# Staging the raw blocks of the key table in PSUM, by quarters, and the dots' fixed rows in four banks

## The reference, cut to what matters

```python
best, sel = lax.top_k(cand, PEER_TOPK)            # 8 heads x 16 experts for each token
eidx = jnp.take_along_axis(cidx, sel, axis=-1)
g = jax.nn.softmax(best, axis=-1)
u = jnp.take(u_tab, eidx, axis=0)
a = jax.nn.gelu(jnp.einsum('thkd,td->thk', u, xb).astype(jnp.float32))
vv = jnp.take(v_tab, eidx, axis=0)
return jnp.einsum('thk,thkd->td', (g * a).astype(xb.dtype), vv)
```

## Time and profile before

| | |
|---|---|
| median of 3 runs | 2502.88 us (2501.28 to 2506.49) |
| the profiled execution, its own time | 2504.55 us |
| its span, first to last instruction | 2503.0 us |
| busy: PE, DVE, POOL, ACT | 2275.1, 1816.6, 1172.0, 938.5 us |
| U stage in the profile | about 801 to 1757 us |
| V stage | about 1757 to 2495 us |

### The profile page before, as it was taken

One profiled execution on the slowest core, in us unless ns is written; L12 is line 12 of the kernel. 1 busy time (PEld: TensorE's weight loads), 2 busy tenths in 40 slices (PEclk: granted clock), 3 DMA queues, 4 the chain that ended last, 5 costly groups with the idle time before them and its releaser, 6 DMA issues.

```text
span 2503.0 us, 36629 instructions
## 1 busy us (share of the span) xinstructions
PE 2275.1 (91%) x13843; PEld 2021.0 (81%) x13843; DVE 1816.6 (73%) x2242; ACT 938.5 (37%) x1030; POOL 1172.0 (47%) x618
## 2 busy tenths in 40 slices
PE   7989999899999999777887878778999999999998
PEld 5878778788899999777887878778877777777777
DVE  3555555563468998878776766676789988998988
ACT  4364553533333443323322222233333333333332
POOL 1020100120005877788887887883444454544441
PEclk9999999999999999989998898889999999999999
DMA  5463444477334678899999999999999999999996
GB/s 186 135 194 119 155 141 126 161 290 294 125 114 135 167 209 290 317 327 323 368 336 323 314 325 321 314 319 341 382 411 413 411 413 412 412 412 409 412 413 278
DMA packets 221520, 722.70 MB, mean 289 GB/s; under 512 B 55672, under 2 KB 105624, under 8 KB 154871
## 3 DMA queue, kind: packets, MB, share of 16 engines
q1 hardware_dynamic: 113872, 380.68, 41.1%
q0 software_dynamic: 87408, 318.89, 35.9%
q10 hardware_dynamic: 20151, 22.05, 2.6%
HBM read 679.70 MB, written 41.83 MB: 288 GB/s over the span
## 4 chain that ended last, share of the span: by engine, by line
PE 34%; POOL 23%; DMA 20%; DVE 13%; issue 8%; DVEq 1%; ACT 1%; SPq 1%; ACTq 0%; POOLq 0%
POOL g_dense L478 16%; PE banks L1331 10%; PE banks L1333 10%; PE banks L1332 10%; DMA v_raw<-in_v_tab 9%; POOL u_row L472 7%; DMA a_tile<-a_dense 7%; DVE h L1275 5%; DMA g_dense<-route,route_place 3%; DVE v_lo L1281 2%; DVE ring_lo L1281 1%; DVEq L832 1%; DVE prm L934 1%; DMA raw<-in_w_in 1%; DVE u_lo L1195 0%
## 5 line engine op out<-in xcount | busy, mean ns | idle before, releaser
L478 POOL DMA_INDIRECT g_dense<-route,route_place x256 | 565.8, 2210 | 304.8 <-DVE route_place L1188 175.9
L1333 PE MATMUL banks<-xT_hi,u_lo 128*128 128x256 f32 x2048 | 600.0, 293 | 0.0
L515 POOL DMA_INDIRECT v_row<-in_v_tab,route_place x128 | 340.2, 2657 | 411.9 <-DVE h L1275 364.8
L1235 DVE CUSTOM_DVE_ANT_0 u_row<-u_row,x_rows 128x2048 f32<-128x2048 f32 x128 | 293.2, 2291 | 195.5 <-DMA u_row<-in_u_tab,route_place 193.8
L1333 PEld LDWEIGHTS banks<-xT_hi,u_lo 128*128 128x128 f32 x2048 | 415.0, 203 | 0.0
L854 DVE TENSOR_TENSOR ring_lo<-raw,ring_hi 128x2048 fp32r<-128x2048 f32 x72 | 165.0, 2291 | 216.0 <-ACT ring_hi L542 215.6
L1275 DVE SCALAR_TENSOR_TENSOR h<-v_row,w_values,h 128x2048 f32<-128x2048 f32 x128 | 300.2, 2345 | 0.7
L1331 PE MATMUL banks<-xT_hi,ring_hi 128*128 128x256 f32 (+1 forms) x768 | 236.0, 307 | 29.4 <-DVE u_lo L1195 29.4
L776 ACT ACTIVATE gelu_out<-gelu_out 128x256 f32<-128x256 f32 x128 | 53.4, 417 | 544.5 <-DVE gelu_out L1229 532.3
L1332 PE MATMUL banks<-xT_lo,ring_hi 128*128 128x256 f32 (+1 forms) x768 | 234.6, 305 | 0.0
L1331 PE MATMUL banks<-ring_hi,w_hi 128*128 128x512 f32 x512 | 204.5, 399 | 19.9 <-DVE ring_lo L1281 18.3
(11 more groups left out here) (264 smaller groups left out, 5522.6 us busy)
## 6 DMA issues: line engine op xcount, KB each, us to landing
v_raw<-in_v_tab SPq DMA_DIRECT2D x128, 1024.0 KB, 14.7
u_raw<-in_u_turned SPq DMA_DIRECT2D x64, 1024.0 KB
raw<-in_u_turned SPq DMA_DIRECT2D x64, 1024.0 KB, 5.8
raw<-in_w_in SPq DMA_DIRECT2D x160, 256.0 KB, 3.5
raw<-in_w_out SPq DMA_DIRECT2D x64, 256.0 KB, 4.4
g_dense<-zeros POOLq DMA_DIRECT2D x16, 1024.0 KB, 28.6
raw<-in_w_pq SPq DMA_DIRECT2D x64, 256.0 KB, 3.6
a_dense<-gelu_out ACTq DMA_DIRECT2D x128, 128.0 KB
```

What stands on the lines that cost most here:

```text
L478: pool.indirect_dma_start(out=places, out_offset=bass.IndirectOffsetOnAxis(ap=routeU[:, t, 2, j:j + 1], axis=0), in_=route[:, t, 0, j:j + ...
L515: pool.indirect_dma_start(out=vrow[k % NVB][:, :], out_offset=None, in_=rows, in_offset=bass.IndirectOffsetOnAxis(ap=routeU[:, NT - 1, 1, ...
L1235: V.tensor_tensor_reduce(row[:, :], row[:, :], xrow[:, :], 1.0, 0.0, ALU.mult, ALU.add, adot[:, i:i + 1]).then_inc(dot_done, 1)
L1333: return MM(out, l1, h2, start=False, stop=last)
```

## The change

ScalarE gets a new step, `u_stage(m)`, right behind `u_hi(m)`: it copies the raw block by quarters of 512 columns into PSUM banks 2 and 3 in turn. VectorE's `u_lo(m)` becomes four instructions, each of which takes one quarter from its bank and the high part from SBUF. ScalarE may write a bank again when VectorE is done with the quarter two before. TensorE waits for the quarters one by one. Since banks 2 and 3 are taken, TensorE accumulates in banks 0 and 1 only, and `scaled(m-2)` stands right behind `u_lo(m)`, ahead of routing and dots, in place of `scaled(m-3)` at the end. Blocks 0 and 1 lose their early place among the last sweeps of the stage before. `x_rows`, the operand that all dots share, is copied once (m = 4) into banks 4 to 7, and the dots read it there.

```diff
+        xbank = psum[:, 4:8, :]
...
+            def u_stage(m):
+
+                for i in range(4 * m, 4 * m + 4):
+                    if i >= 2:
+                        act.wait_ge(u_lo_done, i - 1)
+                    A(bank[2 + i % 2], rawu[m % UR][:, i % 4 * W:(i % 4 + 1) * W], ACT.Copy).then_inc(u_bank, 1)
...
-                act.wait_ge(u_scaled, m + (UR + 1))
+                act.wait_ge(u_scaled, m + 3)
...
+            u_stage(0)
             for m in range(1, P):
                 if m >= 2:
                     u_hi(m)
+                u_stage(m)
...
+                if m == UR:
+                    act.wait_ge(x_row, 1)
+                    A(xbank, xrow[:, :].rearrange("p (b x) -> p b x", x=W), ACT.Copy).then_inc(x_bank, 1)
...
                 dve.wait_ge(u_hi_done, m + 1)
-                V.tensor_tensor(uL[m % UR].rearrange("p (b e) -> p b e", e=P), rawu[m % UR].rearrange("p (b e) -> p b e", e=P),
-                                uH[m % UR].bitcast(F32), ALU.subtract).then_inc(u_lo_done, 1)
+                for i in range(4 * m, 4 * m + 4):
+                    dve.wait_ge(u_bank, i + 1)
+                    V.tensor_tensor(uL[m % UR][:, i % 4 * W:(i % 4 + 1) * W].rearrange("p (b e) -> p b e", e=P),
+                                    bank[2 + i % 2].rearrange("p (b e) -> p b e", e=P),
+                                    uH[m % UR][:, i % 4 * 4:i % 4 * 4 + 4, :].bitcast(F32), ALU.subtract).then_inc(u_lo_done, 1)
...
-                V.tensor_tensor(aout[:, m % 2, :], bank[m % UR][:, 0:TU], rootB[:, :], ALU.mult).then_inc(u_scaled, 1)
+                V.tensor_tensor(aout[:, m % 2, :], bank[m % 2][:, 0:TU], rootB[:, :], ALU.mult).then_inc(u_scaled, 1)
...
-                V.tensor_tensor_reduce(row[:, :], row[:, :], xrow[:, :], 1.0, 0.0, ALU.mult, ALU.add, adot[:, i:i + 1]).then_inc(dot_done, 1)
+                V.tensor_tensor_reduce(row[:, :], row[:, :], xbank.rearrange("p b x -> p (b x)"), 1.0, 0.0, ALU.mult, ALU.add, adot[:, i:i + 1]).then_inc(dot_done, 1)
...
             for m in range(P):
+                u_lo(m)
                 if m >= 2:
-                    u_lo(m)
+                    scaled(m - 2)
...
-                if m >= UR - 1:
-                    scaled(m - (UR - 1))
...
                 pe.wait_ge(u_scaled, m + 1)
-                pe.wait_ge(u_lo_done, m + 1)
                 for b in range(KC):
+                    if b % 4 == 0:
+                        pe.wait_ge(u_lo_done, m * 4 + (b // 4 + 1))
```

More of the change, by code:

```diff
@@ L296, in hybrid_layer @@
         row_used = sem("row_used")
+        u_bank = sem("u_raw_in_bank")
+        x_row, x_bank = sem("x_row_ready"), sem("x_bank_ready")
         urow_in = [sem(f"urow_in{i}") for i in range(NUB)]
@@ L849, in _ @@
             dve.sem_inc(lo_done, 2)
-            dve.sem_inc(u_scaled, UR)
+            dve.sem_inc(u_scaled, 2)
             V.memset(epsv, EPS).then_inc(z_done, 1)
@@ L1212, in _ @@
                     V.scalar_tensor_tensor(out=xrow[:, :], in0=hh[:, NT - 1, :], scalar=rrx[:, NT - 1:NT], in1=gbc[:, :],
-                                           op0=ALU.mult, op1=ALU.mult)
+                                           op0=ALU.mult, op1=ALU.mult).then_inc(x_row, 1)
                     drain()
@@ L1216, in _ @@
                     sweep(n)
-                    if s == 15:
-                        u_lo(i)
                 for quarter, part in QUARTER_IN_PQ.get(s, ()):
@@ L1228, in scaled @@
                     dve.wait_ge(root_ev, 1)
-                V.tensor_tensor(aout[:, m % 2, :], bank[m % UR][:, 0:TU], rootB[:, :], ALU.mult).then_inc(u_scaled, 1)
+                V.tensor_tensor(aout[:, m % 2, :], bank[m % 2][:, 0:TU], rootB[:, :], ALU.mult).then_inc(u_scaled, 1)
             def dot(i):
+                if i == 0:
+                    dve.wait_ge(x_bank, 1)
                 dve.wait_ge(urow_in[i % NUB], 16 * (i // NUB + 1))
                 row = urow[i % NUB]
-                V.tensor_tensor_reduce(row[:, :], row[:, :], xrow[:, :], 1.0, 0.0, ALU.mult, ALU.add, adot[:, i:i + 1]).then_inc(dot_done, 1)
+                V.tensor_tensor_reduce(row[:, :], row[:, :], xbank.rearrange("p b x -> p (b x)"), 1.0, 0.0, ALU.mult, ALU.add, adot[:, i:i + 1]).then_inc(dot_done, 1)
             sweep(3 * N_SWEEPS - 1)
@@ L1281, in v_lo @@
                 V.tensor_tensor(vL[m % VS], vraw[m % VS], vH[m % VS].bitcast(F32), ALU.subtract).then_inc(lo_done, 1)
-            scaled(P - 3)
+            scaled(P - 2)
             v_lo(0)
-            scaled(P - 2)
             w_product(0)
@@ L1583, in u_step @@
                 pe.wait_ge(u_scaled, m + 1)
-                pe.wait_ge(u_lo_done, m + 1)
                 for b in range(KC):
+                    if b % 4 == 0:
+                        pe.wait_ge(u_lo_done, m * 4 + (b // 4 + 1))
                     c = slice(b * P, (b + 1) * P)
-                    last = three(bank[q][:, 0:TU], uH[q][:, b, :], uL[q][:, c], xTh[:, b, 0:TU], xTl[:, b, 0:TU], b == 0, b == KC - 1)
+                    last = three(bank[q % 2][:, 0:TU], uH[q][:, b, :], uL[q][:, c], xTh[:, b, 0:TU], xTl[:, b, 0:TU], b == 0, b == KC - 1)
                 last.then_inc(u_used, 1)
@@ L1606, in v_step @@
                     last.then_inc(split_used, 1)
-            pe.wait_ge(u_scaled, P + UR)
+            pe.wait_ge(u_scaled, P + 2)
             pe.wait_ge(wl_done, 1)
```

## The result

The changed kernel takes 2866.97 us (median of 4 runs, 2855.63 to 2867.47) beside 2504.05 us for the kernel before in the same comparison: a ratio of 1.1445, 95% interval 1.1418 to 1.1471. It is 363 us slower. I had forecast 43 us faster; the slowest of my rivals stood at 2538.

The account below looks back on a forecast made before the run. POOL, its indirect DMAs held by VectorE instructions with two SBUF inputs, was taken to set the U stage's pace from 957 us. Terms +16 - 16 - 43 = -43 us gave a forecast of 2460 us, range 2433 to 2500.

Parts of the forecast that it names:

- ScalarE's round: ScalarE's in-order work per U-stage block: about 5.6 us, under PE's 5.75; blocks with one dot lose 0.2 us.
- the signs that I had listed for being wrong: U stage: POOL's durations stay, DMA's share stays 0.94 with POOL idle, or DVE waits for banks over 0.5 us a quarter.
- To block 26: U stage, 801 to 957 us: dearer low parts 13 us, ScalarE's round some 3 us, together +16 us.
- Blocks 26 to 51: U stage, 957 to 1163 us: DVE's own work plus a few waits for rows makes 190 us, -16 us.
- Blocks 52 to 121: U stage, 1163 to 1708 us: DMA is next to bound, 502 us for 545, -43 us, ends -33 to -62.
- My last rival: DMA has more room than its share says; DVE sets step 3 at 434 us, -111, total 2392 us; chance 0.05.
- the price of the quarters: VectorE's low part of a U-stage block in four quarters through two banks: about 2.7 us, taken as +0.5 us a block.
- two accumulators at next to nothing: U stage: VectorE's lead over PE shrinks from three blocks to two; cost put at nothing.
- The passage of the Trainium skill that I set among the rivals: Supports the rival that the change frees nothing: POOL's durations stay, +16 us or so, 2519 us; chance 0.02.
- the hand-over of quarters: Rival, U stage: low parts cost more than taken; at 1.2 us more a block, +35 us, 2538 us; chance 0.07.
- The rival that DMA is the bound already: U stage: POOL's freedom only moves the wait; step 3 gives 0, Blocks 26 to 51 at most -10; 2509 us; chance 0.09.
- step 3: The forecast's term for Blocks 52 to 121, U stage, 1163 to 1708 us: DMA-bound at 502 us, -43 us.

Follow-up runs that it names:

- experiment 3: The changed kernel with gelu(m-3) between u_hi(m) and u_stage(m) on ScalarE, a block earlier, still two gelu_out buffers: 2404.8 us, ratio 0.9608.
- experiment 8: experiment 3 with the low part of blocks 0 to 25 in one instruction from SBUF, unstaged, as in the kernel before: 2392.6 us, ratio 0.9568.
- experiment 4: The kernel before with only the dots' part: x_rows copied once into banks 4 to 7 and read there by the dots: 2432.8 us, ratio 0.9724.
- experiment 6: experiment 3 with the dots reading x_rows from SBUF again, so the staging without the dots' part: 2491.8 us, ratio 0.9944.
- experiment 5: The kernel before with two accumulators in place of four and scaled(m-2) right behind the low part, no staging: 2494.6 us, ratio 0.9964.
- experiment 9: The changed kernel with the dots' rows in SBUF and four staging banks, gelu behind the staging, two gelu_out buffers: 2481.5 us, ratio 0.9912.

## Why the prediction was wrong

**The step that failed** is the last sentence of "ScalarE's round": "`u_hi(m+1)` is queued behind `u_stage(m)`, and `gelu` too; the gelus wait for nobody's sake." Somebody does wait for them. The store that a gelu ends in frees one of two `gelu_out` buffers, and `scaled` needs it. I named what is queued behind the new wait and did not go on from there to who waits for it. All the pieces were there: `scaled` waits for the store of the block two before its own, the stores stand in the timeline, and the change brings `scaled` one block forward while it puts the gelu behind a wait for VectorE. Its price follows from the trace after: gelu 0.4, issue, and landing, 4.9 us from the gelu's start (1508.77) to `scaled` (1513.69), against 0.8 us that VectorE needs from that start to the end of its low part. That is 4.1 us a block, and 4.1 x 117 = 480 of the 495 us. None of the signs that I had listed for being wrong names the store.

**The sum's other terms** can be read in experiment 3, where that wait is gone (span 2405.8, that is -97 us).
1. To block 26: +23 us for +16. Some 17 us lie between the low parts of block 2 and block 26 (153.8 us for 137.2), near what I counted. The other 6 come at the start: block 2's low part begins at 826.3 for 820.0. I named no cost for the start. VectorE stands still for 8.0 us ahead of block 0's low part, since ScalarE comes to its first copies only behind its work for the scores. In experiment 8, with the same order and nothing staged there, block 2 begins at 822.7. So in these profiles about 3 of the 6 us go with the lost place of blocks 0 and 1 and 4 with the staging.
2. Blocks 26 to 51: 187 us for 210, -23 where I had -16.
3. Blocks 52 to 121: 448 us for 545, -97 where I had -43. I took the DMA share as an amount of work, 0.94 x 545 = 512 us. In experiment 3 the share makes 1.04 x 449 = 467 us, for nearly the same bytes (330 GB/s x 545 us = 180 MB before, 393 x 449 = 176 MB). So the same bytes took more packet time in the kernel before, and the share overstated what was needed. My last rival had this mechanism, with 434 us for this step and 2392 us in all. Experiment 3, at 448 and 2405, is nearer to it than to the forecast's 502 and 2460. Whether DMA or VectorE sets the pace there isn't shown.

**What held:** POOL held by dots and low parts with two SBUF inputs and not by those with one in PSUM (experiments 4 and 6 show each kind by itself); the price of the quarters, 2.65 us for 2.7; and two accumulators at next to nothing (experiment 5). That DMA is next is not shown, as item 3 says. The passage of the Trainium skill that I set among the rivals ("SBUF — State Buffer", section "Who interferes with whom"), by which descriptor generation would be spared by `tensor_tensor`, does not hold here: the scatter of 1314.67 in experiment 4 took 3.12 us against 1.57. The rule of the Trainium skill in the same section, that two SBUF inputs contend with GpSimd's reads, agrees with these traces. The 65 ns that the Trainium skill has for a PSUM source ("VectorE: DVE Perf Modes", section on the TRN2 errata) are not seen: the dot takes 2281 ns from PSUM and took 2291 from SBUF, and the quarter takes 686.

**The rival whose time came nearest**, the hand-over of quarters, had its place right (ScalarE and VectorE coupled by two banks) and its mechanism wrong: VectorE loses next to no time between quarters, 2.65 us for the low part against 2.48 with four banks.

The rival that DMA is the bound already is out: it gave step 3 nothing, and experiment 3 gains 97 us there.

## What to carry to other kernels

When an in-order engine gets a new wait, write down everything behind it in its queue, for each the buffer that it frees, and who writes that buffer next; a store of 128 KB that lands 4.3 us behind its issue (the median here) is enough to close a circle between two engines, and the others stand behind it. If all engines fall to half load at once and the chain names a small transfer, look for such a circle, and give it one more buffer or issue the freeing work ahead of the wait: here 1 KB a partition was worth 428 us and a gelu issued a block earlier 462. GpSimd's indirect DMAs beside long VectorE instructions were cheaper with one operand of each of these in PSUM: for the dots alone that was worth 71 us.

## What the runs showed of the hardware

A DVE instruction was not slowed by a POOL instruction that ran at its start (low parts of the kernel before: 2281 ns on average where one ran, 2286 where none did), but a POOL indirect DMA that started within a low part or a dot with two SBUF inputs stood still to its end: in experiment 4, 57 scatters that started within low parts took 2976 ns on average and 73 that started within dots 1566. So VectorE and GpSimd meet at more than semaphores. The DMA share is no measure of work: 512 us of packets for 180 MB in the kernel before became 467 for 176 MB in experiment 3, and the share rose to 1.04. A ScalarE copy of 512 columns took 0.60 us from SBUF into PSUM, and DVE read four such quarters in 2.65 us through two banks and in 2.48 through four (experiment 9).
